# Token rows of a top-2 expert layer fetched by index from memory, in place of one-hot products

## The chip, the cores and the metric

The kernel runs on one core of one Trainium2 chip, in float32. A core has five engines that run side by side and meet only at semaphores: TensorE (PE, matrix products), VectorE (DVE), ScalarE (ACT), GpSimd (POOL) and SyncE (SP, which here only starts transfers). Sixteen DMA engines move data between the memory (HBM) and the on-chip buffer (SBUF). The products land in PSUM, eight banks of 128 x 512 numbers (`bank`). The metric is the device time of one launch in microseconds.

## What is computed

One decoder layer for 256 prompt tokens and 8 x 4 = 32 sample tokens, 288 tokens (T) of width 2048. The change lies in the expert layer at its end; `h` is the normed token, and 32 experts have three weight matrices each:

```python
def _hier_moe(h, rg_w, rg_b, re_w, re_b, w_gate, w_up, w_down):
    t = h.reshape(B * L, D)
    g_prob = softmax(t @ rg_w + rg_b);  g_val, g_idx = top_k(g_prob, 1)      # one of 4 groups
    e_in = (t @ re_w + re_b).reshape(T, 4, 8)[g_idx]                         # its 8 experts
    e_val, e_idx = top_k(softmax(e_in), 2);  e_val = e_val / sum(e_val)      # two of them
    comb = one_hot(g_idx) * (g_val * within)                                 # weights of T x 32
    act = silu(t @ w_gate[e]) * (t @ w_up[e]) * comb                         # w_gate, w_up: 2048 x 512
    return sum over e of act @ w_down[e]                                     # w_down: 512 x 2048
x = LN2(alpha * x + gate2 * moe)
```

Each token goes to two experts, so there are 576 pairs of token and expert. With this reference's inputs the routing gives the experts 0 to 31 these numbers of rows: 27, 97, 35, 19, 0, 5, 101, 26, 4, 2, 17, 11, 5, 9, 12, 6, 9, 10, 0, 5, 0, 1, 4, 7, 28, 16, 10, 7, 17, 7, 29, 50. One expert's weights are 12 MB, all of them 402.7 million bytes, and each is read once.

## The kernel before

**Blocks.** The rows of an expert are worked on in blocks of 64 slots (`SLOTS`). Every expert has at least one block; experts 1 and 6 have more than 64 rows and so two each. That makes 34 blocks, b0 to b33: b1 and b2 are expert 1, b7 and b8 are expert 6, b(k) is expert k-2 from b9 on. All engines run the same loop over the blocks (`expert_loops`): 32 turns, and then the extra ones, guarded by a count.

**Weights.** `ring` holds 12 chunks of 1 MB, exactly one expert: chunks 0 to 7 are w_gate and w_up in turn, 8 to 11 w_down. SP (`moe_sp`) loads chunk j of expert e as soon as PE has used chunk j in the block before that expert's first one (`used`), so while an expert's first of two blocks runs, nothing can be loaded for the next expert. PE waits for each chunk by itself (`landed[j]`).

**A block on PE** (`moe_pe.body`): 64 products of 128x64 by 128x512 for gate and up (L752, in four groups of 16, each on two chunks); in between, 20 products that pick the rows of the next block out of `H`, where the normed tokens stay in SBUF, by a one-hot matrix `sel` (L732 16 of them, L721 4: "gather"). Then 8 transposes turn the rows that were picked (L740, `turn`), 4 transposes the activations (L764), and 32 products make the down projection (L772). ACT does silu (L676), two copies of the rows and the activations (L666, L671, L679), and half of the result's copy (L682). DVE multiplies gate and up (L603), copies the other halves (L582, L587, L609), makes `sel` for the block after the next (L567, L571) and the row numbers under which the result is stored (L591 to L612). POOL writes the block's result rows to `y_dram`, in slot order, by an indirect DMA (L540); rows beyond an expert's count have a number out of bounds and aren't written.

**Before and after the loop.** POOL fills `y_dram` (40 x 64 rows of 8 KB) once from a constant (L526), since slots that no token has are never written. After the loop POOL reads every token's two result rows back by six indirect DMAs (L798), PE weighs and adds them (L833), and DVE and ACT do the last norm.

Names: `rows_ready`, `xg_ready`, `act_ready`, `at_ready`, `ys_act`, `ys_dve`, `y_row`, `y_written` are semaphores; `XG` the picked rows (128 partitions: 64 slots x 2 halves of a row, 4 KB each), `xT` the same turned, `YS` the result.

## Time and profile before

| | us |
|---|---|
| three runs, median (lowest, highest) | 1746.58 (1746.25, 1747.17) |
| the profiled execution | 1748.22 |
| its span, first to last instruction | 1746.4 |
| first product of b0 (L752) | at 698.3 |
| last product of b33 ends (L772) | at 1693.8 |
| result rows landed, read back, first L833 on them | at 1711.1 |

PE is busy 93% of the span, DVE 30%, ACT 19%, POOL 8%, and the DMA engines moved 597 MB at a mean of 342 GB/s. The expert stage is 995 of the 1746 us. A block there is read in three ways: PE's instructions in order of time, the moments when SP starts the loads of the next expert, and the busy share of the DMA engines in a stretch. In the views, "idle before <-X" names what an engine waited for last; DMA share 1.0 means that all sixteen engines were busy, and PEclk is the granted share of TensorE's clock.

### The profile page before, as it was taken

How to read it: one execution, taken by the hardware profiler on the slowest of the kernel's cores; microseconds unless marked ns; L12 is line 12 of the kernel's file. 1: busy time of each engine (PE TensorE's matmuls, PEld its weight loads, DVE VectorE, ACT ScalarE, POOL GpSimd, SP SyncE). 2: the span in 40 equal slices, each digit the busy share in tenths (PEclk: the TensorE clock that was granted, in tenths of full speed). 3: DMA queues.
4: the chain of work that ended last, by engine and by line, in shares of the span. 5: the costliest groups of instructions: out<-in, count | busy, mean ns of one | idle time of the engine just before them, and what ended most of it. 6: DMA issues, size and time to landing. Idle time of an engine off the chain costs nothing.

```text
span 1746.4 us, 23478 instructions
## 1 busy us (share of the span) xinstructions
PE 1624.3 (93%) x8925; PEld 696.9 (40%) x8926; DVE 518.3 (30%) x1467; ACT 324.3 (19%) x601; POOL 145.2 (8%) x218
## 2 busy tenths in 40 slices
...
GB/s 301 386 369 126 309 289 283 294 151 96 160 273 348 342 375 313 346 259 422 422 375 307 423 421 422 421 422 421 422 421 422 421 421 421 422 421 421 421 238 154
DMA packets 124903, 597.44 MB, mean 342 GB/s; under 512 B 16665, under 2 KB 21561, under 8 KB 65929
## 3 DMA queue, kind: packets, MB, share of 16 engines
...
## 4 chain that ended last, share of the span: by engine, by line
PE 63%; DMA 31%; DVE 3%; ACT 2%; issue 1%; POOL 0%; SPq 0%; POOLq 0%; DVEq 0%; ACTq 0%
DMA ring<-in_exp_w_up 27%; PE bank L752 17%; PE bank L772 6%; PE bank L2325 6%; PE bank L2233 5%; PE bank L2082 4%; PE bank L732 3%; PE bank L338 3%; DMA ring<-in_ada_w 3%; PE bank L2276 2%; PE bank L2165 2%; PE bank L2060 2%; PE bank L833 1%; PE bank L721 1%; PE bank L2072 1%
## 5 line engine op out<-in xcount | busy, mean ns | idle before, releaser
L752 PE MATMUL bank<-ring,BC 128*64 128x512 f32 x2176 | 550.6, 595 | 13.8 <-DMA ring<-in_exp_w_up 12.2
L752 PEld LDWEIGHTS bank<-ring,BC 128*64 128x64 f32 x2176 | 172.9, 137 | 350.3 <-issue 292.0
L772 PE MATMUL bank<-ring,BC 128*64 128x512 f32 x1088 | 241.0, 595 | 15.7 <-ACT BC L679 15.7
L582 DVE COPY MOD<-bank 128x512 f32<-128x512 f32 x35 | 24.2, 692 | 497.0 <-PE bank L721 493.9
L732 PE MATMUL bank<-H,BC 128*64 128x512 f32 x544 | 158.7, 592 | 0.0
L772 PEld LDWEIGHTS bank<-ring,BC 128*64 128x64 f32 x1088 | 75.1, 137 | 156.3 <-issue 135.9
L666 ACT COPY MOD<-bank 128x512 f32<-128x512 f32 x35 | 20.5, 586 | 496.2 <-PE bank L721 472.4
L540 POOL DMA_INDIRECT y_dram<-BC,y_row x34 | 32.9, 967 | 946.3 <-DVE y_row L612 830.1
L2325 PE MATMUL bank<-ring,MT 128*128 128x512 f32 x224 | 102.2, 610 | 1.0 <-issue 0.8
L2233 PE MATMUL bank<-ring,MT 128*128 128x512 f32 x192 | 85.4, 598 | 1.0 <-ACT X L1162 1.0
L732 PEld LDWEIGHTS bank<-H,BC 128*64 128x64 f32 x544 | 48.5, 137 | 77.6 <-issue 77.6
L609 DVE COPY BC<-bank 128x512 f32<-128x512 f32 x34 | 23.5, 692 | 179.9 <-PE bank L772 179.9
L2082 PE MATMUL bank<-MT,ring 128*128 128x288 f32 x256 | 65.8, 420 | 2.3 <-DVE MT L1522 2.3
L682 ACT COPY BC<-bank 128x512 f32<-128x512 f32 x34 | 19.9, 586 | 247.0 <-PE bank L772 247.0
L338 PE MATMUL bank<-ring,cT 128*32 128x512 f32 x512 | 64.1, 616 | 1.0 <-DMA ring<-in_ada_w 1.0
L2325 PEld LDWEIGHTS bank<-ring,MT 128*128 128x128 f32 x224 | 42.4, 194 | 55.1 <-issue 54.4
L603 DVE TENSOR_TENSOR BC<-BC,bank 64x512 f32<-64x512 f32 x34 | 23.5, 692 | 124.9 <-ACT BC L676 124.9
L2082 PEld LDWEIGHTS bank<-MT,ring 128*128 128x128 f32 x256 | 50.2, 198 | 17.3 <-DVE MT L1522 2.4
L2060 PE MATMUL bank<-ring,cT 128*32 128x512 f32 x256 | 40.1, 731 | 16.5 <-DMA ring<-in_ada_w 16.1
L2233 PEld LDWEIGHTS bank<-ring,MT 128*128 128x128 f32 x192 | 35.6, 190 | 48.1 <-issue 46.9
L740 PEld LDWEIGHTS bank<-con,MOD 128*128 128x128 f32 x280 | 36.4, 210 | 28.4 <-issue 27.6
L740 PE MATMUL bank<-con,MOD 128*128 128x128 f32 x280 | 43.0, 297 | 0.7 <-DVE MOD L582 0.7
...
## 6 DMA issues: line engine op xcount, KB each, us to landing
ring<-in_exp_w_gate SPq DMA_DIRECT2D x128, 1024.0 KB, 24.3
ring<-in_exp_w_up SPq DMA_DIRECT2D x128, 1024.0 KB, 26.2
ring<-in_exp_w_down SPq DMA_DIRECT2D x128, 1024.0 KB, 24.7
...
```

The source lines that it names most:

```text
L338: mm = pe.matmul(bank[32 * g:32 * g + 32, b, :], cT[:, k, :], w[:, 512 * g:512 * g + 512], start=(k == 0), stop=(k == KD - 1))
L540: pool.indirect_dma_start(y_dram.rearrange("r (c n) -> (r c) n", c=2), bass.IndirectOffsetOnAxis(ap=y_row[:, :], axis=0), YS[:, :, :].rear ...
L732: pe.matmul(bank[64 * h:64 * h + 64, i, :], sel[:, b, :], H[:, b, 512 * q:512 * q + 512], start=(b == 0), stop=False)
L740: mm = pe.transpose(bank[:, i, P * k:P * k + P], XG[:, i, k:512:4], ident)
L752: mm = pe.matmul(bank[64 * i:64 * i + 64, 2, :], xT[:, q // 2, k % 4, 64 * (q % 2):64 * (q % 2) + 64], ring[:, j, 512 * (k % 4):512 * (k % ...
L772: mm = pe.matmul(bank[64 * (c % 2):64 * (c % 2) + 64, 4 + c // 2, :], aT[:, j, :], ring[:, 8 + j, 512 * c:512 * c + 512], start=(j == 0), ...
L2060: mm = pe.matmul(bank[32 * g:32 * g + 32, 4 + v, :], cT[:, 4 * i + g, :], w[:, g, :], start=(i == 0), stop=(i == 3))
L2082: mm = pe.matmul(bank[:, 4 * half + m, 0:T], w[:, k, P * m:P * m + P], MT[:, 4 * j + k, :], start=(j == 0 and k == 0), stop=(j == 3 and k ...
L2165: mm = pe.matmul(bank[:, X_BANK + q // 2, x:x + NC], BT[c][g, r, m, :], UT[g, m, r, :], start=(r == 0), stop=(r == QC - 1))
L2233: pe.matmul(bank[:, b, :], MT[:, 4 * i + k, P * b:P * b + P], w[:, k, :], start=(i == 0 and k == 0), stop=(i == 3 and k == 3))
L2276: mm = pe.matmul(bank[:, 4 + m % 2, 0:T], w[:, k, P * (m % 2):P * (m % 2) + P], Z[:, k, :], start=(k == 0), stop=(k == 7))
L2325: pe.matmul(bank[:, x, :], MT[:, k0 + k, P * b:P * b + P], w[:, k, :], start=(half == 0 and k == 0), stop=(half == 1 and k == 3))
```

## The change

A block's rows are no longer picked by products. The normed tokens are stored once in memory (`h2_dram`, by SP, 2.4 MB), and the rows of a block are fetched from there by an indirect DMA of POOL straight into `XG` (`fetch`): 128 indices, two halves for each slot, unused ones out of bounds. To know which token has which slot, POOL first scatters the numbers of the 576 pairs into a table in memory (`pair_dram`: one fill, six indirect DMAs of 4-byte elements) and reads it back into SBUF twice (`pairs`); DVE works out of it the columns `x_rows` (where to read) and `y_rows` (where to write), and copies one column for each block. Results go to `y_dram` in the order of token and rank, so that ACT and SP read them back by plain DMAs at the end; the fill of `y_dram` is gone.

```diff
-            for r in range(0, NBLK * SLOTS, P):
-                pool.dma_start(y_dram[r:r + P, :].rearrange("p (i n) -> p i n", i=4), spread_mid(con[:, 0:512], 4))\
-                    .then_inc(S("y_written"), 16)
+            pool.dma_start(pair_dram.rearrange("(s k) o -> s (k o)", s=SLOTS), a["route_consts"][0:SLOTS, R_FILL:R_N])\
+                .then_inc(S("rows_stored"), 16)
+            pool.wait_ge(S("rows_stored"), 16)
+            pool.wait_ge(S("slots_ready"), since("slots_ready") + 1)
+            for b, n in BLK:
+                for k in range(2):
+                    pool.indirect_dma_start(pair_dram, bass.IndirectOffsetOnAxis(ap=slot_i[0:n, b, k:k + 1], axis=0),
+                                            con[0:n, C_PAIR + 2 * b + k:C_PAIR + 2 * b + k + 1], None)\
+                        .then_inc(S("rows_stored"), 16)
+            pool.wait_ge(S("rows_stored"), TABLED)
+            for c in range(2):
+                pool.dma_start(pairs[64 * c:64 * c + 64, :], pair_dram.rearrange("(s k) o -> s (k o)", s=SLOTS))\
+                    .then_inc(S("pairs_in"), 16)
+            def fetch():
+                pool.indirect_dma_start(XG[:, :, :].rearrange("p i n -> p (i n)"), None, h2_rows,
+                                        bass.IndirectOffsetOnAxis(ap=x_row, axis=0),
+                                        bounds_check=2 * T - 1, oob_is_err=False).then_inc(S("rows_in"), 16)
+            def body(e):
+                pool.wait_ge(S("rint_ready"), since("rint_ready") + 3)
+                pool.wait_ge(S("x_row"), e)
+                fetch()
+                pool.wait_ge(S("rint_ready"), since("rint_ready") + 3)
+                pool.wait_ge(S("y_row"), e)
+                pool.indirect_dma_start(y_rows_out, bass.IndirectOffsetOnAxis(ap=y_row, axis=0),
+                                        YS[:, :, :].rearrange("p j n -> p (j n)"), None,
+                                        bounds_check=4 * T - 1, oob_is_err=False).then_inc(S("rows_stored"), 16)
+            pool.wait_ge(S("h2_out"), 128)
+            pool.wait_ge(S("x_first"), since("x_first") + 1)
+            fetch()
             pool.wait_ge(S("x1_ready"), 2)
             pool.dma_start(GE[:, 0, :], a["ln2_g"].to_broadcast([P, D])).then_inc(S("ln2_in"), 16)
...
         def moe_sp(sp):
+            sp.wait_ge(S("hs_ready"), since("hs_ready") + 1)
+            for q in range(4):
+                sp.dma_start(by_halves(h2_dram[SEQ:T, :])[:, q // 2, q % 2, :], H[32 * q:32 * q + 32, 2, 0:512])\
+                  .then_inc(S("h2_out"), 16)
+            sp.wait_ge(S("h2_ready"), 8)
+            for b in range(2):
+                for c in range(2):
+                    sp.dma_start(by_halves(h2_dram[P * b:P * b + P, :])[:, :, c, :],
+                                 H[:, b, :].rearrange("p (j c n) -> p j c n", j=2, c=2)[:, :, c, :]).then_inc(S("h2_out"), 16)
...
             def body(e):
-                rows_out(e + 1)
                 dve.wait_ge(S("sg_ready"), e + 1)
                 V.tensor_tensor(AC[hi, :], SG[hi, :], bank[hi, 2, :], ALU.mult).then_inc(S("act_ready"), 1)
                 turned_out(e + 1)
-                select(e + 2)
-                dve.wait_ge(S("y_written"), Y_FILLED + 16 * e)
-                rows_of(e)
+                dve.wait_ge(S("xg_ready"), 2 * e + 4)
+                V.tensor_copy(x_row, x_rows[:, bass.ds(e + 2, 1)]).then_inc(S("x_row"), 1)
+                dve.wait_ge(S("rows_stored"), TABLED + 16 * e)
                 dve.wait_ge(used, len(plan) + (e + 1) * RING)
...
+            dve.wait_ge(S("pairs_in"), 32)
+            go(V.memset(x_rows[:, NBLK:NBLK + 2], 2 * NO_ROW),
+               V.tensor_scalar(second, pairs, float(T), -2.0 * T, ALU.is_ge, ALU.mult),
+               V.tensor_scalar(y_rows, pairs, 2.0, half, ALU.mult, ALU.add))
+            go(V.tensor_tensor(x_rows[:, 0:NBLK], y_rows, second, ALU.add))
+            dve.wait_ge(S("xg_ready"), 2)
+            V.tensor_copy(x_row, x_rows[:, 1:2]).then_inc(S("x_first"), 1)
...
+            body(0)
             for b in range(2):
                 x = X[:, b, :]
...
-                    if k in (3, 7):
-                        gather_pair(e + 1, k // 4)
-                    elif k == 11:
-                        gather_samples(e + 1)
-                turn(e + 1)
                 pe.wait_ge(S("rint_ready"), since("rint_ready") + 3)
                 pe.wait_ge(S("act_ready"), e + 1)
                 for j in range(4):
                     mm = pe.transpose(bank[:, 3, SLOTS * j:SLOTS * j + SLOTS], AC[hi, j:FE:4], ident[hi, 64:128])
                 mm.then_inc(S("at_ps"), 1)
+                pe.wait_ge(S("rows_in"), 16 * e + 16)
+                turn()
                 pe.wait_ge(S("at_ready"), e + 1)
...
-        def tail_pool(pool):
-            pool.wait_ge(S("y_all"), since("y_all") + 1)
-            for b in F_ORDER:
-                for i in range(2):
-                    rows = y_dram[:, :] if b < 2 else y_dram.rearrange("s (q n) -> (s q) n", q=4)
-                    pool.indirect_dma_start(Y[:, b, i, :] if b < 2 else Yq[i], None, rows,
-                                            bass.IndirectOffsetOnAxis(ap=slot_i[:, b, i:i + 1], axis=0))\
-                        .then_inc(S(f"y_in{b}"), 16)
```

The order of the instructions shows the three places where something moves. On PE, the end of a block before (`turn` at L740 ahead of the activations' transposes at L764, one group of the gather at L721 still among the products):

```order
L752 MATMUL bank<-ring,BC 64x512 [waits landed5]
L752 MATMUL bank<-ring,BC 64x512 x6
L721 MATMUL bank<-H,BC 64x512 x4
L750 REGISTER_ALU
L752 MATMUL bank<-ring,BC 64x512 [waits landed6]
L752 MATMUL bank<-ring,BC 64x512 [waits landed7]
L752 MATMUL bank<-ring,BC 64x512 x6
L737 ISA
L740 MATMUL bank<-con,MOD 128x128 [waits rows_ready]
L740 MATMUL bank<-con,MOD 128x128 x7
L764 MATMUL bank<-con,BC 128x64 [waits act_ready,msq_ready]
L764 MATMUL bank<-con,BC 128x64 x3
```

and now (the lines are those of the changed kernel):

```order
L761 MATMUL bank<-ring,BC 64x512 [waits landed7]
L761 MATMUL bank<-ring,BC 64x512 x6
L768 MATMUL bank<-con,BC 128x64 [waits act_ready,msq_ready]
L768 MATMUL bank<-con,BC 128x64 x3
L770 ISA
L749 MATMUL bank<-con,MOD 128x128 [waits rows_in]
L749 MATMUL bank<-con,MOD 128x128 x7
L778 MATMUL bank<-ring,BC 64x512 [waits ys_dve,landed8,ys_act,at_ready]
```

The gather is gone, the activations' transposes come first, and the turn of the next block's rows stands between them and the down projection, behind a wait for the fetch (`rows_in`). On POOL, from the fill to the loop's first body, before:

```order
L526 DMA y_dram<-con 512x1x512 [waits landed3]
L526 DMA y_dram<-con 512x1x512 x19
L529 DMA GE<-in_ln_g 128x2048 [waits x1_ready]
L530 DMA GE<-in_ln_b 128x2048
L533 DMA X<-in_ln_g 32x512 x4
L533 DMA X<-in_ln_b 32x512 x4
L510 UNCONDITIONAL_BRANCH [waits msq_ready]
L540 DMA y_dram<-BC,y_row 5120x1024 [waits y_row,msq_ready]
```

and now:

```order
L537 DMA pair_dram<-con,slot_i 2560x1 [waits sel_ready,rows_stored]
L537 DMA pair_dram<-con,slot_i 2560x1 x5
L542 DMA MOD<-pair_dram 64x40 [waits rows_stored]
L542 DMA MOD<-pair_dram 64x40
L547 DMA MOD<-h_dram,slot_i 128x1024 [waits sel_ready,h2_out]
L566 DMA GE<-in_ln_g 128x2048 [waits x1_ready]
L567 DMA GE<-in_ln_b 128x2048
L570 DMA X<-in_ln_g 32x512 x4
L570 DMA X<-in_ln_b 32x512 x4
L518 UNCONDITIONAL_BRANCH [waits msq_ready]
L547 DMA MOD<-h_dram,slot_i 128x1024 [waits x_row,msq_ready]
L558 DMA y_dram<-BC,slot_i 1152x1024 [waits y_row,msq_ready]
```

The second fetch (the first L547 behind L518, rows of b2) stands behind the ten loads of the last norm's vectors, which wait for `x1_ready`. On DVE, who gives `x1_ready`, the stretch before the loop, before:

```order
L650 TENSOR_SCALAR MT<-con,cwt 128x128 x5
L653 SCALAR_TENSOR_TENSOR X<-X,st,GE 128x2048
L656 SCALAR_TENSOR_TENSOR X<-X,st,GE 128x2048 [waits dve_self]
L653 SCALAR_TENSOR_TENSOR X<-X,st,GE 128x2048
L656 SCALAR_TENSOR_TENSOR X<-X,st,GE 128x2048 [waits dve_self]
L510 UNCONDITIONAL_BRANCH [waits msq_ready]
```

and now:

```order
L670 MEMSET MOD 128x2 [waits pairs_in]
L671 TENSOR_SCALAR MOD<-MOD 128x40
L672 TENSOR_SCALAR MOD<-MOD,con 128x40
L673 TENSOR_TENSOR MOD<-MOD 128x40 [waits dve_self]
L675 CAST slot_i<-MOD 128x1 [waits xg_ready,dve_self]
L622 TENSOR_TENSOR BC<-BC,bank 64x512 [waits sg_ready,msq_ready,sel_ready]
L617 COPY BC<-bank 128x512 [waits turn_ps]
L625 CAST slot_i<-MOD 128x1 [waits xg_ready]
L628 COPY BC<-bank 128x512 [waits used,rows_stored]
L631 CAST slot_i<-MOD 128x1 [waits ys_act,ys_dve]
L681 SCALAR_TENSOR_TENSOR X<-X,st,GE 128x2048
L684 SCALAR_TENSOR_TENSOR X<-X,st,GE 128x2048 [waits dve_self]
```

All of b0's DVE work now comes ahead of the four updates of X that give `x1_ready`, and it waits for the table (`pairs_in`).

## Rows read from the trace of the kernel before

**Rows 1.** Busy time by stretch: engines (x instructions), PEclk, DMA share, GB/s.

```profile
650.00:660.00 10.00, 9.27 (x31) 4.54 (x31) 8.63 (x22) 3.81 (x10) 0.00 (x0) 1.00 0.77 296
690.00:700.00 10.00, 8.48 (x40) 3.07 (x38) 5.82 (x29) 2.46 (x3) 0.00 (x0) 0.87 0.34 142
...
930.00:1120.00 190.00, 184.16 (x896) 65.44 (x894) 34.50 (x111) 35.36 (x48) 5.77 (x6) 1.00 1.01 418
1120.00:1690.00 570.00, 541.93 (x2492) 192.49 (x2490) 94.87 (x304) 95.10 (x129) 18.27 (x19) 1.00 1.00 415
```

**Rows 2.** Order of time over one block: start, duration, engine, line, [idle before <-releaser].

```profile
1000.26 7.09 PE L772 MATMUL bank<-ring,BC 128*64 128x512 f32 x32 [0.46 <-ACT BC L679]
...
1010.61 1.89 PE L732 MATMUL bank<-H,BC 128*64 128x512 f32 x8
...
1021.01 1.09 PE L721 MATMUL bank<-H,BC 32*64 32x512 f32 x8
...
1022.03 3.65 PE L752 MATMUL bank<-ring,BC 128*64 128x512 f32 x16
...
1025.61 1.23 PE L740 MATMUL bank<-con,MOD 128*128 128x128 f32 x8
...
1026.38 0.69 DVE L603 TENSOR_TENSOR BC<-BC,bank 64x512 f32<-64x512 f32 x1 [3.52 <-ACT BC L676]
...
1027.21 0.66 PE L764 MATMUL bank<-con,BC 64*128 64x64 f32 x4 [0.38 <-DVE BC L603]
...
1028.34 7.09 PE L772 MATMUL bank<-ring,BC 128*64 128x512 f32 x32 [0.46 <-ACT BC L679]
```

**Rows 3.** SP's order of time: first load of experts 1, 2 and 7.

```profile
702.09 0.36 SPq L382 DMA_DIRECT2D ring<-in_exp_w_gate  x1
...
758.25 0.34 SPq L382 DMA_DIRECT2D ring<-in_exp_w_gate  x1
...
926.71 0.34 SPq L382 DMA_DIRECT2D ring<-in_exp_w_gate  x1
```

**Rows 4.** ACT's order of time: the same copy in b20 to b23.

```profile
1292.00 0.37 ACT L679 COPY BC<-bank 128x256 f32<-128x256 f32 x1 [0.42 <-PE bank L764]
...
1321.88 0.37 ACT L679 COPY BC<-bank 128x256 f32<-128x256 f32 x1 [0.40 <-PE bank L764]
...
1352.35 0.37 ACT L679 COPY BC<-bank 128x256 f32<-128x256 f32 x1 [0.41 <-PE bank L764]
...
1382.25 0.37 ACT L679 COPY BC<-bank 128x256 f32<-128x256 f32 x1 [0.40 <-PE bank L764]
```

**Rows 5.** Busy time in short stretches, columns as in rows 1.

```profile
744.00:758.00 14.00, 13.17 (x68) 5.20 (x66) 4.32 (x15) 3.42 (x5) 1.01 (x1) 1.00 0.00 1
...
1676.00:1678.00 2.00, 2.00 (x12) 0.70 (x9) 0.00 (x0) 0.00 (x0) 0.00 (x0) 1.00 0.94 393
...
1688.00:1690.00 2.00, 2.00 (x12) 0.72 (x10) 0.50 (x4) 0.00 (x0) 0.00 (x0) 1.00 0.10 41
```

**Rows 6.** Order of time around b0; then the landing times of L540's writes.

```profile
692.19 0.18 DVE L629 TENSOR_REDUCE X<-H 40x1 f32<-40x32 f32 x1
...
698.27 3.65 PE L752 MATMUL bank<-ring,BC 128*64 128x512 f32 x16 [0.86 <-DVE BC L587]
...
709.70 2.35 DVE L656 SCALAR_TENSOR_TENSOR X<-X,st,GE 128x2048 f32<-128x2048 f32 x1
...
712.35 0.56 POOL L529 DMA_DIRECT2D GE<-in_ln_g  x1 [97.51 <-DVE X L656]
...
DMA to landing us min/median/max: 3.3/7.7/9.8
```

**Rows 7.** Order of time at the end of the loop and behind it.

```profile
1693.86 0.69 DVE L609 COPY BC<-bank 128x512 f32<-128x512 f32 x1 [5.29 <-PE bank L772]
...
1699.17 1.00 POOL L798 DMA_INDIRECT ring<-y_dram,slot_i  x1 [2.60 <-ACTq L695]
...
1711.09 9.88 PE L833 MATMUL bank<-ring,MT 128*128 128x512 f32 x16 [3.27 <-DMA ring<-y_dram,slot_i]
```

163 lines of the change are left out of this document (71 added, 92 removed).

## The prediction

> **What bounds the kernel now.** I read the stretches first [rows 1], then PE's order of time over one block [rows 2], then when SP starts an expert's loads [rows 3], and last how the DMA engines end a run of loads [rows 5]. From 930 us on the DMA engines are full (share 1.01 and 1.00), and PE is nearly full too (184.2 of 190, 541.9 of 570). So the two are close, and the reader has to find out which one comes last, and when. In [rows 2] a block takes 1028.34 - 1000.26 = 28.08 us and PE waits for no load: PE sets the pace. In [rows 4], later, the distance from block to block is 29.88, 30.47 and 29.90 us, and PE's instructions are the same: there the loads set it. The change takes work from PE. That helps only where PE sets the pace.
>
> Where is that? Between 744 and 758 us the DMA share is 0.00 [rows 5]: the ring holds expert 1, which has two blocks, and nothing can be loaded until b2 uses chunk 0. The same happens before 926.71, where b8, the second block of expert 6, frees the ring for expert 7 [rows 3]. Up to 926.71 the path therefore goes through PE; from there 25 experts are loaded without a pause, and this chain of loads, not PE, ends the stage. That b9 to b15 still run at 28.08 us only uses up the lead of a full ring.
>
> **What the loads' pace is made of.** The blocks of [rows 4] are b20 to b23, with 0, 5, 0 and 1 rows. A block's result is written while the next one runs. After a block with 0 rows the distance is 29.9 us, after one with 5 rows 30.47, and the ten distances from b23 to b33 (b33's L679 is at 1693.86 - 7.09 - 0.46 = 1686.3) have a mean of 30.40 with 1, 4, 7, 28, 16, 10, 7, 17, 7 and 29 rows written [rows 4, 7]. The cost of a write is thus 0.57 us, whether it has 5 rows or 29: not bytes over all engines (17 rows of 8 KB are 0.14 MB, 0.33 us at 418 GB/s [rows 1]), but bytes on the busiest engine. A second sign is how the loads end: the share falls slowly, from 0.94 at 1676 us to 0.10 at 1688 us [rows 5], so one engine is some 12 us behind another, about the 22 writes with rows since 927 us times 0.57. Four rows of 4 KB are 16 KB; an engine moves 418/16 = 26.1 GB/s, 0.63 us. So I count 0.145 us a row up to four rows, no more up to 32, and the same again beyond (0.57 / 4 = 0.143).
>
> [...]
>
> **The change, part by part.**
>
> *Before b0.* The fill ends by 660 us (share 0.77 from 650 on) and PE was 93% busy there without waiting for loads, while expert 0's loads still come in time for 698.27 [rows 1, 6]: its removal gives 0. `h2_dram`'s 2.4 MB (5.6 us at 418 GB/s) are stored after 692 us, when the engines are nearly idle (share 0.34) [rows 1]; 0 for PE.
>
> *A block on PE.* L752's last product ends at 1022.03 + 3.65 = 1025.68. The gather goes: 2 x 1.72 (8 products, 1.89 with an overlap of 0.17) + 1.02 (1.09 less 0.07) = 4.46 us. The products of gate and up are 1025.68 - 1007.35 - 4.46 = 13.87 us. Before, `turn` (1.23) hid silu and L603; now they stand open: L764 starts 1027.21 - 1025.68 = 1.53 after the products. Then L764 0.66, turn 1.23 (it hides the copy L679 that cost 0.46), and the down projection 7.09. New block: 24.4 us in place of 28.08 [rows 2]. PE waits on `rows_in` only if the fetch is late. In the loop it isn't: it is issued in the block before, some 24 us ahead, and an indirect write lands after 7.7 us (9.8 at most) [rows 6].
>
> *The start.* b0's turn would come at 698.27 + 13.87 + 1.53 + 0.66 = 714.3. Its rows need a chain: slot numbers at about 692.5 (they take L629's place) [rows 6], six scatters of 1.0 us and 0.3 between (L798's time [rows 7]), 7.7 us, to 700.2; landed 3.3 us later, 703.5; two table reads, 1.1 to issue and 3.3 to 7.7 to land, 710; five small DVE steps, 1 us; the fetch, 7.7 to 9.8: **719.5**, so PE waits 5 us (0 if all land at the lower end, 17 if all take 9.8). b0 ends at 719.5 + 1.23 + 7.09 = 727.8. Then comes what the order shows: POOL's second fetch stands behind `x1_ready`. DVE updates X only after b0, 0.7 + 4 x 2.35 = 10.1 us, 738; POOL issues ten loads, ten times half a microsecond [L529, rows 6], 743; the fetch lands after 3.3 to 4.5 since no expert is loading: **747.3**. b1's turn would be at 727.8 + 16.1 = 743.9: 3.4 us of waiting (0 to 9). b1 ends at 755.6, and expert 2's loads begin at 755.6 + 3.43 + 0.3 = 759.3, against 758.25 [rows 3]: **1 us later**. Two blocks saved 7.4 us, the two waits and the lost table time took it.
>
> *Experts 2 to 6.* With 24.4 us of PE, loads set the pace from here. 5 x 29.9 = 149.5; writes of b1 to b6 (64, 33, 35, 19, 0, 5 rows) 1.16 + 0.72 + 1.0 + 0.57 + 0 + 0.57 = 4.0; fetches of b4 to b8 (19, 0, 5, 64, 37) 3.5, if they cost what writes cost: 157.0. b7 ends 3 us behind the last load, and b8's first group takes 3.4 + 0.3: expert 7's loads begin at 759.3 + 157 + 3.3 + 3.7 = 923.3, against 926.71 [rows 3]: **-3.4 us**.
>
> *Experts 7 to 31.* Before, from 926.71 to 1693.86 [rows 3, 7]. The 24 fetches of b10 to b33 come on top: 19 with four to 29 rows 10.8, two rows 0.29, one row 0.14, none 0, and 50 rows 1.16: **+12.5 us**. The trace of before has no fetch under load; its bounds are 0 (it falls on other engines, which have up to 12 us of slack) and twice a write, 25 us. I take one write, since both are indirect, 4 KB a row, over the same 128 partitions.
>
> *The end.* ACT's four plain loads are issued at once where POOL needed 1.3 us for each of six, but they stand ahead of ACT's copies of gate2 by some 2 us, and 4.7 MB still take 11 us. L833's 1711.09 comes 1 to 2 us earlier at best, and the DVE chain behind it is unchanged: **-1.5** (-3 to +1).
>
> Sum: -3.4 + 12.5 - 1.5 = +7.6, and 1 us for b9's write and the 50-row fetch falling together at the end: span 1746.4 + 8.6 = 1755.0. The profiled execution took 1748.22 with this span, 1.64 above the median; so 1755.0 + 1.8 - 1.64 = **1755.2 us** for a median run.
>
> **Rivals.** (1) The fetch is free: its rows fall on engines with slack, so periods stay 30.47. For it: mean load grows only 0.33 us a block. Against it: same partitions, same kind. Then 12.5 + 3.5 us go: about 1740 us, faster. It decides from a fetch cost of 0.2 us a block downwards. (2) The fetch costs twice a write, because reads of scattered rows hold the engine for both directions, or the table's many small packets delay b0 to the upper bound (17 us): 1755 + 12 to 16, about 1769. (3) The fill was not hidden: expert 0's and the last `w_out` loads shared the engines with it. PE's gaps were 0.7 us in the 10 us before 660 [rows 1]; with as much in every 10 us since 600, 4 us go: 1751, and together with part of rival 1 about 1747. (4) PE waits 6 us in each block and its clock falls. Before, PEclk read 1.00 where PE was 93% busy and 0.87 where it was 85% [rows 1]; now it will be 24.4 of 31.0, 79%. [...] The waits are short, since a pair of chunks lands every 5 us and each pair gives 3.4 us of work.
>
> [...] No row of this case has waits of this kind in every block.
>
> **How the numbers follow.** Forecast (one write's price a fetch) 0.58, 1749 to 1762. Rival 1: 0.22, 1736 to 1744. Rival 2: 0.12, 1762 to 1775. Rival 3: 0.04. Rival 4: 0.04. The range of 8 in 10 takes the forecast, most of rival 1 and half of rival 2: 1739 to 1768. A measurement can tell about 0.2%, 3.5 us, from no change. Faster (below 1743.1): 0.2, nearly all of rival 1; within: 0.14, its upper edge, rival 3 and the forecast's lowest end; slower (above 1750.1): 0.66.
>
> **What would show it.** Distance of blocks in the loaded part: 31.0 us after blocks with four rows and more if the forecast holds, 30.47 if rival 1 does, 31.6 if rival 2. PE's idle time in front of `turn`: about 5 and 3 us in b0 and b1, none later. First load of expert 2 at 759, of expert 7 at 923. The DMA share at the end of the loads falls over some 24 us in place of 12. PEclk 1.00 through the stage. The forecast is wrong if DMA engines other than those of the writes serve the fetch, or if one of the three landings in b0's chain takes much more than 8 us.

## The result, and the profile after

The changed kernel took a median of 1777.35 us in four runs (1771.99 to 1777.88), the kernel before beside it 1746.88: a ratio of 1.0161, 95% interval 1.0144 to 1.0177. The prediction had said 1755.2, with 1768 as its upper end. The sign is right, the loss 30.5 us where 8.6 had been forecast. A second measurement of both gave 1774.0 us and 1.0137 (1.0114 to 1.0159), a loss of 24.7 us. The profiled execution of the changed kernel took 1771.99 us, with a span of 1770.1.

The stretches first (busy time of PE, PEld, DVE, ACT and POOL with their numbers of instructions, then PEclk, DMA share and GB/s):

```profile
700.00:760.00 60.00, 43.02 (x196) 16.62 (x194) 14.27 (x20) 4.96 (x8) 10.45 (x16) 0.86 0.74 276
...
930.00:1120.00 190.00, 165.30 (x726) 61.72 (x724) 15.81 (x34) 23.06 (x34) 13.11 (x13) 0.96 1.00 413
1120.00:1690.00 570.00, 463.44 (x1995) 164.32 (x1992) 43.87 (x93) 60.82 (x90) 38.37 (x38) 0.99 1.01 419
...
1694.00:1698.00 4.00, 3.04 (x14) 1.19 (x16) 0.00 (x0) 0.00 (x0) 0.00 (x0) 1.00 0.30 127
...
1702.00:1706.00 4.00, 2.50 (x13) 1.20 (x10) 0.69 (x1) 0.85 (x2) 0.00 (x0) 1.00 0.14 57
```

Beside [rows 1], PE has lost its work: 463.4 busy us of 570 in place of 541.9. The DMA engines are as full as before. Since the loads fill the engines there with or without the gather, its removal had little to win. And from 700 to 760 PE is busy in 43.0 of 60 us: something waits at the start. The share of the DMA engines now falls over some 20 us (it is full up to 1690 us, 0.30 at 1694, 0.14 at 1702, and the last block ends at 1714), where it had fallen over 12 [rows 5].

A block without waits for loads, PE's order of time (start, duration, engine, line, what it waited for), to be held against [rows 2]:

```profile
811.90 13.90 PE L761 MATMUL bank<-ring,BC 128*64 128x512 f32 x64
827.33 0.66 PE L768 MATMUL bank<-con,BC 64*128 64x64 f32 x4 [1.53 <-DVE BC L622]
827.92 1.23 PE L749 MATMUL bank<-con,MOD 128*128 128x128 f32 x8
829.08 7.09 PE L778 MATMUL bank<-ring,BC 128*64 128x512 f32 x32
```

The next block's first product is at 836.00, so a block takes 24.1 us (before 28.08; predicted 24.4). The 1.53 us for silu and the product behind it stand open in every block, as predicted. What PE waited for in the whole span (us in all, times, longest):

```profile
PE bank L761 <- DMA ring<-in_exp_w_up: 109.6, 90, 1.7
PE bank L768 <- DVE BC L622: 51.4, 34, 1.8
...
PE bank L749 <- DMA MOD<-h_dram,slot_i: 13.6, 2, 8.6
...
PE bank L839 <- DMA ring<-y_dram: 7.0, 1, 7.0
```

The gather's time on PE has become 109.6 us of waiting for weights. The fetch is waited for twice only, in b0 and b1, and L839, the sum of the results, waits 7 us. The two waits of the fetch in PE's order of time:

```profile
712.73 0.66 PE L768 MATMUL bank<-con,BC 64*128 64x64 f32 x4 [1.80 <-DVE BC L622]
722.00 1.98 PE L749 MATMUL bank<-con,MOD 128*128 128x128 f32 x8 [8.61 <-DMA MOD<-h_dram,slot_i]
723.92 7.63 PE L778 MATMUL bank<-ring,BC 128*64 128x512 f32 x32
...
752.51 1.98 PE L749 MATMUL bank<-con,MOD 128*128 128x128 f32 x8 [5.03 <-DMA MOD<-h_dram,slot_i]
```

Behind the first wait the eight transposes take 1.98 us in place of 1.23 and the products 7.63 in place of 7.09, behind the second 1.98 and 7.74: TensorE comes back at half its clock (PEclk reads 0.50 from 716 to 724 us and 1.00 from 726 on; 0.50 from 749 to 755 and 1.00 from 756 on). POOL's order of time shows the chain that the rows need; the two lines behind it are the landing times (min/median/max) of L537's scatters and of L542's reads:

```profile
691.65 1.07 POOL L537 DMA_INDIRECT pair_dram<-con,slot_i  x1 [100.73 <-DVE slot_i L644]
...
698.04 0.87 POOL L537 DMA_INDIRECT pair_dram<-con,slot_i  x1 [0.30 <-issue]
705.01 1.13 POOL L542 DMA_DIRECT2D MOD<-pair_dram  x2 [6.11 <-DMA pair_dram<-con,slot_i]
712.75 1.09 POOL L547 DMA_INDIRECT MOD<-h_dram,slot_i  x1 [6.61 <-DVE slot_i L675]
742.15 0.59 POOL L566 DMA_DIRECT2D GE<-in_ln_g  x1 [28.30 <-DVE X L684]
...
747.51 1.07 POOL L547 DMA_INDIRECT MOD<-h_dram,slot_i  x1 [0.30 <-issue]
```

```profile
DMA to landing us min/median/max: 6.0/6.8/7.7
```

```profile
DMA to landing us min/median/max: 5.3/5.4/5.5
```

SP's first loads of experts 2 and 7, to be held against [rows 3]:

```profile
765.76 0.33 SPq L387 DMA_DIRECT2D ring<-in_exp_w_gate  x1
...
932.68 0.33 SPq L387 DMA_DIRECT2D ring<-in_exp_w_gate  x1
```

One thing in this chain differs from what the prediction assumed. It stored `h2_dram` on engines that were "nearly idle"; before, they were (share 0.01 from 694 to 702 us). Now they are full while the scatters are issued, and again when the first fetch is:

```profile
690.00:698.00 8.00, 6.18 (x36) 2.53 (x34) 2.98 (x15) 2.71 (x5) 4.86 (x5) 0.94 1.03 378
...
706.00:722.00 16.00, 5.59 (x28) 2.04 (x24) 1.37 (x6) 0.96 (x2) 1.24 (x2) 0.78 1.01 420
```

How much of the landing times comes from this load no run separates.

And the end of the stage, several engines in order of time, to be held against [rows 7]:

```profile
1713.93 0.69 DVE L628 COPY BC<-bank 128x512 f32<-128x512 f32 x1 [6.04 <-PE bank L778]
...
1716.27 1.00 POOL L558 DMA_INDIRECT y_dram<-BC,slot_i  x1 [6.50 <-issue]
1719.63 4.14 SPq L808 DMA_DIRECT2D ring<-y_dram  x8
1719.67 2.44 ACTq L724 DMA_DIRECT2D ring<-y_dram  x4
...
1733.08 3.75 PE L839 MATMUL bank<-ring,MT 128*128 128x512 f32 x4 [6.98 <-DMA ring<-y_dram]
```

From the last block's copy to the first L839 there are 19.15 us; before, the comparable step to L833 for the samples was at 1704.06, 10.2 us behind the copy at 1693.86.

**One measure for all kernels.** The time at which the first gather (the products at L737, before L709) starts differs from one profiled execution to the next, between 685.6 and 694.1 us, with no relation to the kernel: the two executions of the changed kernel have 687.36 and 688.91, the kernel before 688.82. It is set in the stages ahead of the change, and its cause is open. So I count every kernel's stage from there, in four legs: to SP's first load of expert 2 (A), from it to the first load of expert 7 (B), from it to the last block's copy (C), from it to the end of the span (D). All in us, each from one profiled execution:

| kernel | A | B | C | D | sum |
|---|---|---|---|---|---|
| before | 69.4 | 168.5 | 767.2 | 52.5 | 1057.6 |
| after | 78.4 | 166.9 | 781.3 | 56.2 | 1082.7 |
| after, once more | 78.6 | 166.7 | 781.8 | 56.3 | 1083.4 |
| after, slots spread (e1) | 82.2 | 164.3 | 770.3 | 54.3 | 1071.0 |
| after, fetch twice (e2) | 78.6 | 170.3 | 798.2 | 56.6 | 1103.7 |
| after, fetch moves nothing (e7) | 78.4 | 163.1 | 768.8 | 56.1 | 1066.4 |
| after, norm loads later (e4) | 72.0 | 166.9 | 781.5 | 56.4 | 1076.7 |
| after, no wait for the table (e8) | 74.4 | 166.9 | 781.5 | 56.6 | 1079.3 |
| after, small reads first (e5) | 78.9 | 167.0 | 781.3 | 51.2 | 1078.3 |
| before, slots spread (e3) | 69.7 | 168.5 | 761.3 | 52.4 | 1051.9 |
| the same again (e12) | 69.6 | 168.5 | 762.5 | 51.7 | 1052.2 |
| after, four mends (e10) | 75.8 | 166.6 | 770.7 | 51.6 | 1064.6 |
| mended, b1 gathered by products (e11) | 65.0 | 164.9 | 770.8 | 51.8 | 1052.5 |
| fetch up to b9, then products (e13) | 65.0 | 166.7 | 763.4 | 50.4 | 1045.4 |

The change costs 25.1 us: +9.0 in A, -1.6 in B, +14.1 in C, +3.7 in D. Most legs that an edit doesn't touch repeat within 0.7 us; the same kernel differs once by 1.2 in C (e3 and e12). Leg D of e1, where only the last write is touched, is 1.9 us shorter than after's, and 1.2 of that are the first 20 products of the final sum (10.49 in place of 11.66 us). So a difference below some 2 us in C or D alone is not read as an effect; this is still sharper than the medians.

### The profile page after: what moved, and what is told of

It reads as the page before. It is cut to its first block, busy times and chain, and to the rows that moved or that the text cites. A ratio compares the mean times of both kernels' runs of the same rounds, so it can differ in the third digit from the quotient of the medians.

```text
span 1770.1 us, 21468 instructions
## 1 busy us (share of the span) xinstructions
PE 1506.6 (85%) x8109; PEld 660.4 (37%) x8110; DVE 427.9 (24%) x1087; ACT 263.2 (15%) x535; POOL 168.8 (10%) x236
## 4 chain that ended last, share of the span: by engine, by line
PE 49%; DMA 44%; DVE 3%; issue 1%; ACT 1%; POOL 0%; SPq 0%; POOLq 0%; DVEq 0%; ACTq 0%
DMA ring<-in_exp_w_up 40%; PE bank L761 10%; PE bank L2331 6%; PE bank L2239 5%; PE bank L2088 4%; PE bank L778 3%; PE bank L343 3%; DMA ring<-in_ada_w 3%; PE bank L2171 2%; PE bank L2282 2%; PE bank L2066 2%; PE bank L839 1%; PE bank L2078 1%; DMA MOD<-h_dram,slot_i 1%; PE bank L2334 1%
## 5 line engine op out<-in xcount | busy, mean ns | idle before, releaser
L761 PE MATMUL bank<-ring,BC 128*64 128x512 f32 x2176 | 526.3, 597 | 110.9 <-DMA ring<-in_exp_w_up 109.6
L778 PE MATMUL bank<-ring,BC 128*64 128x512 f32 x1088 | 257.4, 628 | 0.0
L702 ACT ACTIVATE BC<-bank 64x512 f32<-64x512 f32 x34 | 20.0, 589 | 568.4 <-PE bank L761 568.4
L547 POOL DMA_INDIRECT MOD<-h_dram,slot_i x35 | 36.0, 1027 | 695.0 <-DVE slot_i L625 688.1
L628 DVE COPY BC<-bank 128x512 f32<-128x512 f32 x34 | 23.5, 692 | 218.2 <-PE bank L778 218.2
L768 PE MATMUL bank<-con,BC 64*128 64x64 f32 x136 | 22.5, 285 | 51.4 <-DVE BC L622 51.4
L749 PE MATMUL bank<-con,MOD 128*128 128x128 f32 x280 | 47.3, 317 | 14.3 <-DMA MOD<-h_dram,slot_i 13.6
L558 POOL DMA_INDIRECT y_dram<-BC,slot_i x34 | 34.0, 999 | 212.8 <-DVE slot_i L631 191.4
L768 PEld LDWEIGHTS bank<-con,BC 64*128 64x128 f32 x136 | 18.8, 209 | 80.4 <-issue 80.4
L617 DVE COPY BC<-bank 128x512 f32<-128x512 f32 x35 | 24.2, 692 | 87.1 <-PE bank L749 87.1
## 6 DMA issues: line engine op xcount, KB each, us to landing
ring<-in_exp_w_down SPq DMA_DIRECT2D x128, 1024.0 KB, 24.7
```

The costliest lines, as they stand in the source:

```text
L547: pool.indirect_dma_start(XG[:, :, :].rearrange("p i n -> p (i n)"), None, h2_rows, bass.IndirectOffsetOnAxis(ap=x_row, axis=0), bounds_ch ...
L749: mm = pe.transpose(bank[:, i, P * k:P * k + P], XG[:, i, k:512:4], ident)
L761: mm = pe.matmul(bank[64 * i:64 * i + 64, 2, :], xT[:, q // 2, k % 4, 64 * (q % 2):64 * (q % 2) + 64], ring[:, j, 512 * (k % 4):512 * (k % ...
L768: mm = pe.transpose(bank[:, 3, SLOTS * j:SLOTS * j + SLOTS], AC[hi, j:FE:4], ident[hi, 64:128])
L778: mm = pe.matmul(bank[64 * (c % 2):64 * (c % 2) + 64, 4 + c // 2, :], aT[:, j, :], ring[:, 8 + j, 512 * c:512 * c + 512], start=(j == 0), ...
```

## Experiments

My theory before these runs: from expert 7 on, the loads set the time, and a fetch is paid on the busiest DMA engine, as a write is. Rivals: only its bytes count, or it has a fixed price. For what the prediction had missed, the theory was a chain at the start and an order of reads at the end.

**The changed kernel again.**

> The changed kernel as it is, once more, as the measure for the runs beside it: 1777 us (1772 to 1778), ratio to the kernel before 1.016.

Measured: 1774.0 us (1772.22 to 1778.24), ratio 1.0137 (1.0114 to 1.0159). It is within the run-to-run spread of the first result, and it is the measure for the next three, which ran beside it.

**Slots spread over the partitions (e1).**

```diff
-    c[:, C_IOTA:C_IOTA + SLOTS] = np.arange(SLOTS)
+    c[:, C_IOTA:C_IOTA + SLOTS] = np.arange(SLOTS) // 4 + np.arange(SLOTS) % 4 * 16
...
-                pool.dma_start(pairs[64 * c:64 * c + 64, :], pair_dram.rearrange("(s k) o -> s (k o)", s=SLOTS))\
-                    .then_inc(S("pairs_in"), 16)
+                for r in range(4):
+                    pool.dma_start(pairs[64 * c + r:64 * c + 64:4, :],
+                                   pair_dram.rearrange("(r s k) o -> r s (k o)", r=4, s=16)[r])\
+                        .then_inc(S("pairs_in"), 16)
```

> The changed kernel with the slots of a block laid over all 64 partitions of a half (slot s in partition 4*(s%16) + s//16) instead of from partition 0 upwards; the table is read by eight transfers instead of two, which costs the start 1 to 2 us. Busiest-engine theory: the first four slots no longer share one DMA engine; the most rows on one engine are n/8 rounded up instead of 4. Over the 25 experts from expert 7 on that is 7.1 us instead of 13.2 for the writes and as much for the fetches, so -12 us there, -2 us in experts 2 to 6: about 1764 us, distance of loaded blocks 30.5 instead of 31.1. Mean-bytes theory (the rows cost only their bytes over 16 engines): no gain, 1777 to 1779 us. Fixed-price theory (each indirect transfer costs its handling, whatever rows it has): no gain either.

Measured: 1761.21 us, ratio 1.0054 (1.0035 to 1.0072), 12.8 us less than the kernel beside it. In leg C these are the same bytes and the same number of transfers, only on other partitions, and it is 11.0 to 11.5 us shorter (12.2 expected). Both rivals had said none. Some of the gain is lost again at the very end: the last block's down projection takes 8.63 us in place of 7.09, and nothing hides it. Where the forecast was a little off is the start: leg A is 3.7 us longer, not 1 to 2.

**The fetch moves nothing (e7).** From the second fetch on every index is out of bounds, so that the transfer is issued and waited for, but brings no row.

```diff
-                V.tensor_copy(x_row, x_rows[:, bass.ds(e + 2, 1)]).then_inc(S("x_row"), 1)
+                V.tensor_copy(x_row, x_rows[:, NBLK:NBLK + 1]).then_inc(S("x_row"), 1)
```

> The changed kernel whose fetches from the second on get an index out of bounds for every row, so that they are issued and waited for but move no row (the results of all blocks but the first two are wrong). Busiest-engine theory: the price of the fetches goes, 13 us from expert 7 on and 3 us in experts 2 to 6: 1761 us, distance of loaded blocks 30.5. Mean-bytes theory: 292 + 157 rows of 8 KB at 418 GB/s, 9 us less: 1768. Fixed-price theory: unchanged, 1777. If PE's waits set the pace instead (its products, silu and turn now in a row), also unchanged, 1777.

Measured: 1758.27 us, ratio 1.0049 (1.0036 to 1.0062): 15.7 us less. Leg C loses 12.5 us (13.0 against the second execution), the term of the prediction, leg B 3.8 (3.5 predicted). PE's waits for silu are still there, and what else the change costs in leg C is small: at 768.8 it is 1.6 us longer than before, and its blocks take 30.00 and 30.53 us where before they took 29.9 and 30.47. The cause of this remainder is open.

**The fetch twice (e2).**

```diff
                 fetch()
+                pool.indirect_dma_start(H[:, 0, 0:1024], None, h2_rows,
+                                        bass.IndirectOffsetOnAxis(ap=x_row, axis=0),
+                                        bounds_check=2 * T - 1, oob_is_err=False).then_inc(S("pairs_in"), 16)
...
                 dve.wait_ge(S("xg_ready"), 2 * e + 4)
+                dve.wait_ge(S("pairs_in"), 32 + 16 * e)
```

> The changed kernel with every fetch from the second on issued a second time, into a buffer that nothing reads; PE doesn't wait for the second copy. Busiest-engine theory: each block pays another 0.145 us a row up to four rows: +13 us from expert 7 on, +3 in experts 2 to 6, 1793 us, distance of loaded blocks 31.6. Mean-bytes theory: +9 us, 1786. Fixed-price theory: 32 more fetches of the same price as the first 32, +12 us also for blocks with no rows.

Measured: 1792.38 us, ratio 1.0240 (1.0217 to 1.0264): 18.4 us more. Leg C grows by 16.9, somewhat more than the 13 expected; 2.4 us of it lie in two of the last blocks (distances of 32.2 and 33.0 us ahead of the last one, where after has 31.2 and 31.6). Four kernels side by side, ACT's copy in b12 and b13 in the loaded stretch, where the blocks have four rows and more. After:

```profile
1055.61 0.37 ACT L704 COPY BC<-bank 128x256 f32<-128x256 f32 x1 [1.57 <-PE bank L768]
1086.77 0.37 ACT L704 COPY BC<-bank 128x256 f32<-128x256 f32 x1 [1.57 <-PE bank L768]
```

The fetch moves nothing:

```profile
1048.52 0.37 ACT L704 COPY BC<-bank 128x256 f32<-128x256 f32 x1 [1.57 <-PE bank L768]
1079.05 0.37 ACT L704 COPY BC<-bank 128x256 f32<-128x256 f32 x1 [1.57 <-PE bank L768]
```

The fetch twice:

```profile
1060.31 0.37 ACT L708 COPY BC<-bank 128x256 f32<-128x256 f32 x1 [1.57 <-PE bank L772]
...
1092.08 0.37 ACT L708 COPY BC<-bank 128x256 f32<-128x256 f32 x1 [1.57 <-PE bank L772]
```

Slots spread:

```profile
1059.54 0.37 ACT L706 COPY BC<-bank 128x256 f32<-128x256 f32 x1 [1.57 <-PE bank L770]
1089.88 0.37 ACT L706 COPY BC<-bank 128x256 f32<-128x256 f32 x1 [1.57 <-PE bank L770]
```

The distances are 31.16, 30.53, 31.77 and 30.34 us. So no, one and two fetches are 30.53, 31.16 and 31.77: 0.63 and 0.61 us a fetch (0.57 predicted). And the shortest distances, of blocks without rows, are 30.0 us in all four, where the kernels without a fetch have 29.9: an indirect transfer with no valid row costs at most 0.1 us. That excludes a fixed price of the size of a write's.

How the loads end tells on how many engines the price falls. With two fetches the share stays at 0.13 for 10 us, which is two of sixteen engines (0.125):

```profile
1716.00:1726.00 10.00, 7.22 (x32) 3.17 (x32) 1.54 (x3) 1.55 (x3) 0.00 (x0) 0.92 0.13 55
```

**The kernel before with its slots spread (e3, e12).**

```diff
-    c[:, C_IOTA:C_IOTA + SLOTS] = np.arange(SLOTS)
+    c[:, C_IOTA:C_IOTA + SLOTS] = np.arange(SLOTS) // 4 + np.arange(SLOTS) % 4 * 16
-    r[:, R_W] = NO_ROW + 2 * (i % SLOTS) + i // SLOTS
+    r[:, R_W] = NO_ROW + 2 * (i % SLOTS // 4 + i % 4 * 16) + i // SLOTS
```

> The kernel before (gather by products) with the slots of a block laid over all 64 partitions of a half, as in the run on spread slots of the changed kernel; only two tables of constants differ. Busiest-engine theory: the writes cost 7.1 us instead of 13.2 from expert 7 on, and 1 us less in experts 2 to 6 at most: 1740 us, ratio 0.996. Mean-bytes theory: 1747 us, unchanged.

Measured: 1742.04 us, ratio 0.9961 (0.9946 to 0.9975). Two tables of constants, no instruction more or less, and leg C is 5.9 us shorter (6.1 expected). The bytes' rival falls here too. And the loads now end at once, over 4 us in place of 12:

```profile
1684.00:1686.00 2.00, 1.54 (x9) 0.67 (x10) 1.77 (x9) 0.37 (x1) 0.00 (x0) 1.00 0.75 311
1686.00:1688.00 2.00, 2.00 (x12) 0.72 (x10) 0.56 (x4) 0.00 (x0) 0.00 (x0) 1.00 0.25 102
```

No engine is far behind the others any more. The repetition:

> The kernel before with spread slots once more, beside the two mended kernels on the same chip: ratio 0.996 as in its first run.

Measured: 1740.81 us, ratio 0.9956 (0.9939 to 0.9973); leg C is 4.7 us shorter. ACT's copy in b30 to b33, behind blocks with 17, 7 and 29 rows:

```profile
1591.02 0.37 ACT L679 COPY BC<-bank 128x256 f32<-128x256 f32 x1 [0.41 <-PE bank L764]
1621.34 0.37 ACT L679 COPY BC<-bank 128x256 f32<-128x256 f32 x1 [0.41 <-PE bank L764]
1651.35 0.37 ACT L679 COPY BC<-bank 128x256 f32<-128x256 f32 x1 [0.41 <-PE bank L764]
1681.75 0.37 ACT L679 COPY BC<-bank 128x256 f32<-128x256 f32 x1 [0.41 <-PE bank L764]
```

The distances are 30.32, 30.01 and 30.40 us, where the kernel before had 30.48, 30.42 and 30.43. With the slots spread the price follows the number of rows, one step for every eight: over the loaded blocks of this execution the distance is 29.9 us after no row, 30.0 after 4 to 7, 30.14 to 30.19 after 9 to 16, 30.32 after 17 and 30.4 after 28 or 29. That is the row price of the prediction with n/8 rows, rounded up, on the busiest engine.

The new places of the slots, four partitions apart, rest on an estimate of mine, that eight engines then share the rows of each transfer; no row of before shows it. The gains agree with it: 11.0 to 11.5 us in e1 for the 12.2 worked out from it, and 5.9 in e3 for 6.1, for indirect transfers in both directions, most of whose rows are out of bounds.

**The start: the loads of the last norm later (e4).**

```diff
             fetch()
+            body(1)
             pool.wait_ge(S("x1_ready"), 2)
             pool.dma_start(GE[:, 0, :], a["ln2_g"].to_broadcast([P, D])).then_inc(S("ln2_in"), 16)
...
-            expert_loops(pool, body, 1)
+            expert_loops(pool, body, 1, 1)
```

> The changed kernel with the ten loads of the second normalisation's scale and shift issued on POOL after the second fetch and the first write instead of ahead of them. My theory of the start: b1's turn then waits 0 us instead of 5.0, since its rows are asked for at about 732 us instead of 747.5, and expert 2's loads begin up to 5 us earlier, of which the span keeps it all: 1772 us. Rival: the wait is taken over by another (the clock, the loads of expert 2 that can't start before b1 ends anyway, or the ring's lead that is used up in experts 2 to 6), so that under 2 us remain.

Measured: 1765.12 us, ratio 1.0107 (1.0086 to 1.0128), leg A 6.4 us shorter, the others unchanged: the span keeps it all. The second fetch on POOL and SP's first load of expert 2:

```profile
723.16 1.03 POOL L547 DMA_INDIRECT MOD<-h_dram,slot_i  x1 [11.59 <-DVE slot_i L626]
```

```profile
757.54 0.34 SPq L387 DMA_DIRECT2D ring<-in_exp_w_gate  x1
```

b1's wait is gone. The 6.4 us are the 5.0 of the wait and the 1.4 that the low clock behind it had cost (PEclk 0.50; 1.98 for 1.23 and 7.74 for 7.09). The expected 5 us had left the clock out.

**The start: no wait for the table (e8).** The first fetch takes a constant index with 128 valid rows in place of b1's true one (so b1 works on other rows), from a tile of its own, and goes ahead of the table's reads:

```diff
+            pool.wait_ge(S("h2_out"), 128)
+            pool.wait_ge(S("xg_ready"), 2)
+            fetch(x_const[:, 0:1])
             for c in range(2):
                 pool.dma_start(pairs[64 * c:64 * c + 64, :], pair_dram.rearrange("(s k) o -> s (k o)", s=SLOTS))\
...
             pool.wait_ge(S("x_first"), since("x_first") + 1)
-            fetch()
```

> The changed kernel whose first fetch (b1's rows) takes an index that is a constant, 128 valid rows as many as the true one has, so that it doesn't wait for the table's way through memory (the rows of b1 are wrong). It is issued when the scatters have landed and h2 is stored, at 705 us instead of 712.75. My theory of the start: b0's turn waits 1 us instead of 8.6, and 7 us go in the end: 1770 us. Rival: b1's turn, whose rows are asked for only behind the ten loads on POOL, takes the gain back in part: then its wait grows from 5 us, or the ten loads move too; under 3 us remain.

Measured: 1771.08 us, ratio 1.0125 (1.0108 to 1.0143), which overlaps the changed kernel's; leg A 4.0 us shorter, between what the theory (7) and the rival (under 3) had said. The 8.6 us of waiting in b0 are gone, b1's 5.1 remain, and a new wait came that neither had named:

```profile
722.34 0.71 PE L771 MATMUL bank<-con,BC 64*128 64x64 f32 x4 [5.34 <-DVE BC L624]
```

DVE's arithmetic on the table stands ahead of b0's product with silu in its queue. Where the table lands later, because the fetch is issued ahead of its reads, DVE holds PE up even though PE needs nothing from the table: 5.34 us in place of 1.80. In e1 the same wait was 4.16 us: 2.4 of the 3.7 us by which its leg A grew. Most of the rest is the clock, whose price behind the two waits for rows was 4.0 us in e1 and 2.7 in the changed kernel.

**The end: the small reads first (e5).**

```diff
                     sp.dma_start(Yq[k][32 * q:32 * q + 32, :], y_dram[T * k + SEQ:T * k + T, y_cols(q)]).then_inc(S("y_in2"), 16)
+            for b in range(2):
+                for k in range(2):
+                    sp.dma_start(Y[:, b, k, :], y_dram[T * k + P * b:T * k + P * b + P, :]).then_inc(S(f"y_in{b}"), 16)
...
-                    act.dma_start(Y[:, b, k, :], y_dram[T * k + P * b:T * k + P * b + P, :]).then_inc(S(f"y_in{b}"), 16)
```

> The changed kernel with the four big reads of the results at the end issued by SP behind the eight small ones of the samples, instead of by ACT at the same time. My theory of the end: the small reads land 3 us after issue instead of 7.5 to 9.6, PE's sum of the samples starts 3 to 5 us earlier (1728 instead of 1733 us on the trace's time), the big reads are issued 3.6 us later and land as much later, and the span gets 1 to 4 us shorter: 1774 us. Rival: the last block of results ends the span and the big reads' delay eats the gain: 1777 to 1780.

Measured: 1769.77 us, ratio 1.0120 (1.0102 to 1.0138), leg D 5.0 us shorter. The issue of the small reads and PE's first sum behind them:

```profile
1726.87 3.60 SPq L805 DMA_DIRECT2D ring<-y_dram  x8
...
1732.24 3.68 PE L839 MATMUL bank<-ring,MT 128*128 128x512 f32 x4 [1.37 <-DMA ring<-y_dram]
```

5.4 us from issue to sum, in place of 1733.08 - 1719.63 = 13.5. Counted from the last block's copy the first sum comes 8.1 us earlier, more than the 3 to 5 expected. The big reads start 3.6 us later, PE then waits 2.2 us for the first of them, and 5.0 of the 8.1 us are left at the end, where 1 to 4 had been expected. The edit also takes the four issues away from ACT, whose copies of gate2 come 2.5 us earlier for it; what the order alone is worth was not measured.

**All of it together (e10).** e1, e4 and e5, and in addition:

```diff
                 V.tensor_tensor(AC[hi, :], SG[hi, :], bank[hi, 2, :], ALU.mult).then_inc(S("act_ready"), 1)
+                if between:
+                    between()
```

where `between` is the table's arithmetic, in b0 alone.

> The changed kernel with four mends together: slots spread over the partitions, the ten normalisation loads behind the second fetch, the small reads of the end ahead of the big ones, and DVE's table arithmetic moved behind b0's product with silu (in the run on spread slots PE waited 4.2 us for that product). If the effects add: from the start of the gather to the end 1082.7 - 13.6 (spread: loads 11.0, experts 2 to 6 2.6) - 6.4 (loads later) - 5.0 (end) = 1057.7 us, as much as the kernel before with its 1057.6: ratio 1.000. Rival: they overlap, because a stage that gets shorter meets the next limit; then 1.003 or more.

Measured: 1752.29 us, ratio 1.0021 (1.0006 to 1.0035). The sum is 1064.6, not 1057.7: the rival holds. Legs C and D are within 0.4 us of what was expected. B is 166.6, 2.3 us more than in e1, and the cause is open. A is 75.8 in place of 72.0, since the open wait only moved back to the fetch:

```profile
731.41 1.98 PE L754 MATMUL bank<-con,MOD 128*128 128x128 f32 x8 [12.29 <-DMA MOD<-h_dram,slot_i]
```

The eight reads take 3.9 us to issue where two took 1.1, and b0's fetch comes that much later.

**b1 gathered by products as well (e11).** `select` and `gather` run a second time, for slots 64 to 127, behind b0's products of gate and up; the first fetch is b2's.

```diff
+            go(V.tensor_scalar(rsm[:, 4, :, 0:2], slot_f[:, :, :], -float(SLOTS), None, ALU.add))
+            select(1)
...
+                if first:
+                    gather(1)
                 pe.wait_ge(S("rint_ready"), since("rint_ready") + 3)
                 pe.wait_ge(S("act_ready"), e + 1)
...
-                pe.wait_ge(S("rows_in"), 16 * e + 16)
+                if first:
+                    pe.wait_ge(S("rows_ready"), 4)
+                else:
+                    pe.wait_ge(S("rows_in"), 16 * e)
```

> The mended kernel whose second block b1 is gathered by one-hot products too (the second half of the products with silu open stands beside them), so that the first fetch is b2's and no fetch waits for the table: neither b0 nor b1 waits for rows. From the start of the gather to expert 2's first load 66 to 68 us instead of 71.9 (before 69.4), the whole 1052 to 1054 us from the gather's start: ratio 0.996, level with the kernel before with spread slots. Rival: the table, now read while b0 runs, or the extra work on DVE and ACT costs it again: 1057 and ratio 1.000.

Measured: 1742.13 us, ratio 0.9964 (0.9951 to 0.9977), sum 1052.5, leg A 65.0: as the theory said. With that the fully fetching kernel is level with the kernel before with spread slots (1051.9 and 1052.2). PE in b0:

```profile
709.79 3.61 PE L745 MATMUL bank<-H,BC 128*64 128x512 f32 x16
713.33 1.09 PE L749 MATMUL bank<-H,BC 32*64 32x512 f32 x8
714.35 0.69 PE L778 MATMUL bank<-con,BC 64*128 64x64 f32 x4
```

The gather fills the time for which PE would wait for silu anyway, so that the gather's 4.6 us cost PE some 3, and the 12.3 us of waiting of e10 are gone.

**Fetch where PE sets the pace, products where the loads do (e13).** Up to b9 the rows are fetched, from b10 on `gather` stands in every block behind the products of gate and up, with `sel` made by DVE again (`FETCHED` is 9).

```diff
-            with eng.Fori(start + done, start + E) as it:
+            with eng.Fori(start + done, FETCHED) as it:
                 body(it)
+            if between:
+                between()
+            body = late
+            with eng.Fori(FETCHED, start + E) as it:
+                body(it)
...
+                if late:
+                    gather(e * 3 + (10 - 3 * FETCHED))
```

> The mended kernel with both first blocks gathered by products, whose fetches serve the blocks up to b9 alone (where PE sets the pace); from b10 on, where the loads set it, the rows are gathered by one-hot products again, all of them behind the products of gate and up. If a fetch's price lies on the busiest DMA engine and a product's on PE, each is now paid where it is hidden: from the gather's start to expert 2's loads 65.0 us and to expert 7's 164.9 more, as in the run with both first blocks gathered, from there to the last block 762.5 us and 51.7 to the end, as in the kernel before with spread slots: 1044 us in all, against 1057.6 before, ratio 0.992, about 1734 us. Rival: the extra DVE work and products in a row make a block longer than the 30 us of its loads, or the 8 us of fetches in the loaded stretch are replaced by another wait: then 1050 us or more, ratio 0.996.

Measured: 1733.74 us (1730.59 to 1737.46), ratio 0.9921 (0.9903 to 0.9940), 13.3 us faster than the kernel before, and 1045.4 from the gather's start, where 1044 had been expected. Of the 12.2 us less than before, 5.4 to 5.7 are what the spread slots give alone (e3, e12); the rest comes with fetching the first blocks' rows and with the mends. The stretch in which the loads set the pace:

```profile
930.00:1120.00 190.00, 183.07 (x878) 66.41 (x875) 30.09 (x85) 18.43 (x34) 6.90 (x7) 1.00 1.01 422
```

PE is as busy as before (183.1 against 184.2), at full clock, and it costs nothing since the loads need 30 us a block. The block at which it switches was chosen for this input's routing, in which the last expert with two blocks is expert 6; a kernel for any routing would need to decide that from the counts.

## Why the prediction was right or wrong

**What bounds the kernel: right.** PE up to expert 7's loads, the loads from there on. The change won 1.6 us in leg B and nothing in C, though it took 4 us of PE's work out of every block.

**The block on PE: right**, 24.1 us for 24.4, no wait for rows in the loop. **The fill stays open.** The gather starts at 687.4 and 688.9 us without it and at 688.8 with it, but its start varies by more than 8 us between executions, more than the 4 us of rival 3. No run put the fill alone back or took it away.

**The price of a fetch: right in mechanism and size.** 12.5 us predicted, 12.5 measured in leg C by taking the rows away; the period 31.1 for 31.0; the loads end over some 20 us, for the 24 predicted. That the price lies on the busiest engine was an inference then, and that two engines serve the first four slots stood in no row of before. The runs show both: the share of 0.13 at the end of e2 is two engines of sixteen, and other partitions alone take away 11.0 to 11.5 us of leg C in e1 and 4.7 to 5.9 us in e3 and e12. Behind 5, 28 and 29 written rows the kernel before has distances of 30.47, 30.46 and 30.43 us; with the same bytes on spread slots (e12) they are 30.01, 30.43 and 30.40. This was the term with a range of 0 to 25 us, and it is the one that held. The row price in it (0.145 us a row up to four rows, no more up to 32, the same again beyond) had no row of before for its steps; e7, and the changed kernel less e7, have them. In e7 the distance is 30.0 us behind no row, 30.13 behind one written row, 30.25 behind two, 30.54 behind four (b25) and 30.47 to 30.57 behind 5 to 29. Against e7's the changed kernel's distances are 0.55 and 0.66 us longer with fetches of 28 and 29 rows, and 1.21, 1.16 and 1.20 with 37, 50 and 64. Where between 29 and 37 rows the second step comes no run shows. The 1 us that the sum added for b9's write and the 50-row fetch is not confirmed: 1.6 us remain in e7, where that fetch brings no row.

**The start failed: +9.0 us in leg A where the steps said +1.** In the profile's own times, in which the gather starts 1.5 us earlier: b0's turn at 722.00, not 719.5; expert 2's loads at 765.76, not 759.3. The mis-sized terms, in their order:
- "landed 3.3 us later": the scatters took 6.0 to 7.7 us. I had taken the least landing of a result write for a transfer of 4-byte elements, because it was small. The engines weren't idle either, as said above; how much each of the two did is open. The first fetch then landed after 9.2 us, inside its range.
- "the fetch lands after 3.3 to 4.5" in b1, issued at 743: it was issued at 747.5 and landed 5.0 us later, so the turn came at 752.5, not at 747.3. The ten loads themselves took the 5 us I gave them; DVE's update and everything before it had slid.
- The clock. After each wait the turn and part of the down projection ran at PEclk 0.50, 1.3 and 1.4 us more. The term wasn't there at all.

Beneath it lies a choice: I set the chain at one value inside its bounds (5 us of waiting, bounds 0 and 17) and moved on. With 8.6 and 5.0 us the waits are inside those bounds, but the range of the whole was drawn from the fetch's price, and gave the late table only a part of rival 2's 0.12.

**Experts 2 to 6: 2.9 us short.** 164.0 us predicted (759.3 to 923.3), 166.9 measured. The fetches in it are right (3.8 for 3.5, e7); the other 2.6 us are there without them and weren't taken apart further.

**The end failed: -1.5 predicted, +3.7 measured.** The step was "ACT's four plain loads are issued at once, ... 4.7 MB still take 11 us". I counted the bytes and who issues them, and not their order: before, the samples' rows were read first and by themselves, and PE and DVE worked on them while the rest came. In the changed kernel the eight small reads are issued over 4.1 us beside four of 1 MB, and land after up to 9.6 us (median 7.5). With the small reads first (e5) the leg is 51.2 us, 1.3 less than before, about what the term had said.

Together: 6.5 us at expert 2's loads, 2.9 in B, 0.5 in C, 5.2 in D make the 15.1 us between the predicted span 1755.0 and 1770.1. The remaining 7 us to the median lie in no step: 5.4 of them are that the profiled execution was the lowest of its four runs, 1.6 that I had assumed it to be above the median, as the one of before was.

**The rivals.** Rival 1, a free fetch, is excluded by e7 and e2. Rival 3 is the fill, left open above. Rival 2 gave 1769, nearest to the span, for two reasons: a double price, which is wrong, and a late table, which is right in part. Rival 4, the clock, did not come true as a cost: in [rows 1]'s stretches PEclk is 0.96 and 0.99, and in 9 of 26 blocks after 930 us the 32 products of the down projection take 7.94 to 8.78 us in place of 7.09, inside PE's 7 us of slack. Outside the loaded part it did cost: 1.3 and 1.4 us behind the two waits of the start, and 1.5 us in e1's last block (8.63 for 7.09, PEclk 0.66 from 1699 to 1704 us). PE waits about three times 1.3 us for loads in each loaded block, and the clock mostly stays up all the same.
